# C probabilities turned by VectorE and a DRAM scratch array in all four halves, rows centred a pair ahead, rotations reordered

## What is computed

```python
h = x @ w_in                                  # split in ten column groups
a_out = pool_mixer(a_v, a_group_w, a_scale) * silu(a_gate)
b_out = sliding_window_attention(rope(b_q), rope(b_k), b_v, sinks) * silu(b_gate)
# C: 8 heads of 64; a chunk of 64 rows sees itself and the 8 chunks before it
s = (c_q @ c_k.T) * 64 ** -0.5 + rel_bias[h, clip(t - s, -128, 128)]
c_out = softmax(s) @ c_v * silu(c_gate)
y = concat(a_out, b_out, c_out) @ w_out
x = layer_norm(2 ** 0.5 * x + y) * ln_gain + ln_bias   # mean and deviation over the row
```

## Time and profile before

| | |
|---|---|
| median of three runs | 2816.25 us |
| the profiled execution | 2820.24 us, its span 2818.4 us |
| TensorE matmuls busy | 2783.0 us, 99% of the span |
| VectorE, ScalarE, GpSimd busy | 1827.0, 1271.7, 1278.3 us |
| granted clock of TensorE, mean | 0.997 |
| DMA moved | 427.09 MB, 152 GB/s over the span |
| chain that ended last | PE 88%, DVE 6%, DMA 3%, issue 1%, SPq 1%, ACT 1% |

### The profile page before, as it was taken

The page is one execution under the profiler, slowest core; times in us unless marked ns, Lnnn a source line. Parts: engine busy times, 40 slices in busy tenths (PEclk is TensorE's granted clock), DMA queues, the critical chain, the costliest instruction groups (busy, mean ns, idle before and its releaser), DMA issues.

```text
span 2818.4 us, 41183 instructions
## 1 busy us (share of the span) xinstructions
PE 2783.0 (99%) x12996; PEld 2322.1 (82%) x12996; DVE 1827.0 (65%) x2950; ACT 1271.7 (45%) x2628; POOL 1278.3 (45%) x927
## 2 busy tenths in 40 slices
PE   9999999999999999999999999999999999999998
PEld 7888888888888888888887878888888788788886
DVE  5666679623777777862267777896146778778625
ACT  4444466523444445652244445654234444456521
POOL 4444444444344434444444444444444444344441
PEclk9999999999999999999999999999999999999999
DMA  6555432355566533235577775334466777532442
GB/s 213 166 166 160 133 89 82 113 174 182 170 175 174 167 92 101 86 94 178 172 208 200 206 204 148 87 86 124 161 213 198 202 206 215 143 97 83 137 157 102
DMA packets 418502, 427.09 MB, mean 152 GB/s; under 512 B 215424, under 2 KB 256416, under 8 KB 414624
## 3 DMA queue, kind: packets, MB, share of 16 engines
q1 hardware_dynamic: 414544, 409.22, 49.4%
q10 hardware_dynamic: 3792, 15.73, 1.4%
HBM read 348.21 MB, written 79.78 MB: 152 GB/s over the span
## 4 chain that ended last, share of the span: by engine, by line
PE 88%; DVE 6%; DMA 3%; issue 1%; SPq 1%; ACT 1%; POOL 0%; DVEq 0%; ACTq 0%; POOLq 0%
PE acc L725 60%; PE sc L725 18%; PE pv L725 9%; DMA pt_raw<-c_prob_scratch 2%; PE sc L813 1%; DMA raw<-in_wall 1%; DVE mixl L1715 1%; DMA c_prob_scratch<-prob 1%; PE sc L769 1%; DVE res L1882 1%; DVE res L1891 1%; DVE mixh L1715 1%; DVE res L1894 1%; DVE pt L1715 0%; SPq L503 0%
## 5 line engine op out<-in xcount | busy, mean ns | idle before, releaser
L1682 POOL TENSOR_TENSOR wl<-raw,wh 128x512 fp32r<-128x512 f32 x920 | 1277.5, 1392 | 1496.8 <-ACT wh L1151 1486.7
L1151 ACT ACTIVATE wh<-raw 128x512 fp32r<-128x512 f32 x920 | 574.8, 630 | 1089.4 <-PE acc L725 747.5
L725 PE MATMUL acc<-xh,wh 128*128 128x512 f32 x2560 | 1007.7, 394 | 6.8 <-DVE mixl L1715 3.1
L725 PE MATMUL acc<-xh,wl 128*128 128x512 f32 x2560 | 998.3, 390 | 0.0
L725 PE MATMUL acc<-xl,wh 128*128 128x512 f32 x2560 | 998.2, 390 | 0.0
L725 PEld LDWEIGHTS acc<-xh,wh 128*128 128x128 f32 x2560 | 481.7, 188 | 103.7 <-DVE mixl L1715 4.4
L725 PEld LDWEIGHTS acc<-xh,wl 128*128 128x128 f32 x2560 | 480.9, 188 | 103.3
L725 PEld LDWEIGHTS acc<-xl,wh 128*128 128x128 f32 x2560 | 482.0, 188 | 92.3
L1715 DVE TENSOR_TENSOR xl<-prob,xh 128x512 f32 x48 | 55.9, 1165 | 237.3 <-ACT xh L1151 237.3
L725 PE MATMUL sc<-wh,mixh 128*128 128x512 f32 x496 | 193.5, 390 | 0.1
L725 PE MATMUL sc<-wl,mixh 128*128 128x512 f32 x496 | 193.0, 389 | 0.0
(11 more groups left out here) (233 smaller groups left out, 3724.4 us busy)
## 6 DMA issues: line engine op xcount, KB each, us to landing
raw<-in_wall SPq DMA_DIRECT2D x920, 256.0 KB, 2.7
res_scratch<-res ACTq DMA_DIRECT2D x12, 1024.0 KB, 4.2
res<-res_scratch SPq DMA_DIRECT2D x12, 1024.0 KB, 5.2
c_prob_scratch<-prob SPq DMA_DIRECT2D x64, 160.0 KB, 3.0
pt_raw<-c_prob_scratch SPq DMA_DIRECT2D x16, 640.0 KB, 5.0
res<-in_x SPq DMA_DIRECT2D x8, 1024.0 KB, 6.6
x_scratch<-res SPq DMA_DIRECT2D x8, 1024.0 KB, 5.2
x_t_scratch<-turned SPq DMA_DIRECT2D x128, 64.0 KB, 2.6
```

Of the source, the lines that this page charges most:

```text
L725: return nc.tensor.matmul(o, lhsT, rhs, start=start, stop=stop)
L1151: return nc.scalar.activation(o, i, ACT.Copy, scale=scale)
L1682: nc.gpsimd.tensor_tensor(wl[:, s, :], raw[:, s, :], wh[:, s, :].bitcast(F32), ALU.subtract).then_inc(w_lo, 1)
```

## The change

`on_tensor` is false for every half, so that half 1 runs `pair` and `second_half` with the scratch array (there with `turn_rows`, and `bias_rows` in ScalarE's `pair`). From pair 1 on, `load_ln` is issued at unit 1 in place of 8, and `centre` of pair p + 1 stands at the end of pair p; it waits for the sums alone, and `gain` for gain and bias. In the tail the rotations, the parts and the sums are reordered: in a second half `c_lo(2)` and `c_add(1)` now come after the first rotation rather than ahead of it, and `c_lo(3)` after the keys; in a first half `c_lo(3)` comes ahead of the second rotation. `rotated_keys` is the wait and the `keys_lo` that stood there before; the product of the C tail, and the parts made of it, come after the transpose of the B values.

```diff
@@ def on_tensor(it)
-            return it == 1
+            return False
@@ SyncE, pair_events
-                    if s == 8 and it:
-                        sp.wait_ge(w_used, unit(it, p * U_C) + (1 + RING))
+                    if it and s == (1 if p and not on_tensor(it) else 8):
+                        if s == 8:
+                            sp.wait_ge(w_used, unit(it, p * U_C) + (1 + RING))
                         load_ln(it - 1, p)
@@ ScalarE, pair
                     slot(12)
+                    if it == 1:
+                        bias_rows(1, p, tz_second)
@@ ScalarE, tail of a second half
                     c_hi(it, last, 2)
+                    query_hi()
                     split(it, KV0 + 7, 3)
-                    query_hi()
...
                     split(it, KV0 + 9, 1)
+                    b_keys_hi()
                     split(it, KV0 + 10, 2)
                     c_hi(it, last, 3)
                     split(it, KV0 + 11, 3)
-                    b_keys_hi()
...
                     b_query(it, 1, 1)
-                    mix_hi(nb + 2 * C_PAIRS, last + MIX_C)
...
                 split(it, B0 + 7, 3)
+                if not on_tensor(it):
+                    mix_hi(nb + 2 * C_PAIRS, last + MIX_C)
@@ VectorE
             def centre(it, n):
-                dv.wait_ge(ln_in, n * 48 + (192 * it + 48))
+                dv.wait_ge(ln_in, n * 48 + (192 * it + (16 if n and not on_tensor(it + 1) else 48)))
...
-            def gain():
+            def gain(it, n):
+                dv.wait_ge(ln_in, n * 48 + (192 * it + 48))
@@ first_half(p)
-                    if it:
+                    if it and p == 0:
                         centre(it - 1, p)
...
                     gate_ready(p * 2 + ((2 * C_PAIRS + B_TILES) * it + 2), 1)
+                    if it and p + 1 < C_PAIRS:
+                        centre(it - 1, p + 1)
@@ second_half(p)
-                    centre(it - 1, p)
+                    if p == 0:
+                        centre(it - 1, p)
                     low_keys(p)
-                    gain()
+                    gain(it - 1, p)
                     bias()
+                    if turns(it):
+                        turn_rows(it - 1, p)
                     low_values(p)
...
                     c_normalise(it, p, 2)
+                    if p + 1 < C_PAIRS:
+                        centre(it - 1, p + 1)
@@ VectorE, tail
                 rotate(it, 0, KV0 + 3, 0)
-                if not on_tensor(it):
-                    c_add(it, p, 2)
-                rotated_query(ROTS * it + 1, 0)
-                if half(it) and not on_tensor(it):
-                    c_lo(it, p, 3)
-                rotate(it, 1, KV0 + 7, 1, 1.0)
-                if not half(it):
-                    c_lo(it, p, 3)
...
+                elif half(it):
+                    c_lo(it, p, 2)
+                    c_add(it, p, 1)
+                    rotated_query(ROTS * it + 1, 0)
+                    rotate(it, 1, KV0 + 7, 1, 1.0)
+                    c_add(it, p, 2)
+                    rotated_keys()
+                    c_lo(it, p, 3)
+                else:
+                    rotated_query(ROTS * it + 1, 0)
+                    c_add(it, p, 2)
+                    c_lo(it, p, 3)
+                    rotate(it, 1, KV0 + 7, 1, 1.0)
+                    rotated_keys()
+                rotate(it, 2, B0 + 3, 1, source=q_bank)
                 if not on_tensor(it):
-                    c_tail_product(p, C_PAIRS * (it + 1))
-                dv.wait_ge(prod_ok, MIXES * it + 2 * C_PAIRS + 2)
+                    c_add(it, p, 3)
                 rotated_query(ROTS * it + 3, 1)
                 dv.wait_ge(w_used, unit(it, B0 + 7) + (1 + RING))
                 V.transpose(vals, v_bank).then_inc(vt_ok, 1)
                 if not on_tensor(it):
+                    c_tail_product(p, C_PAIRS * (it + 1))
+                    dv.wait_ge(prod_ok, MIXES * it + 2 * C_PAIRS + 2)
                     mix_lo(nb + 2 * C_PAIRS, p + MIX_C)
```

More of the change, by code:

```diff
@@ L2155, in _ @@
                     c_normalise(it, p, 3)
-                    c_lo(it, p, 2)
-                    c_add(it, p, 1)
                 elif not half(it):
@@ L2163, in _, with rotated_keys @@
                     c_lo(it, p, 2)
+                def rotated_keys():
+                    if half(it):
+                        dv.wait_ge(hist_mv, layer(it) + 1)
+                    dv.wait_ge(qh_ok, ROTS * it + 2)
+                    keys_lo([k[:, HD:] for k in bkl], s0[:, 0:HALF], [k[:, HD:] for k in bk]).then_inc(bq_ok, 1)
                 dv.wait_ge(rope_in, 32 * (it + 1))
                 rotate(it, 0, KV0 + 3, 0)
-                if not on_tensor(it):
-                    c_add(it, p, 2)
@@ L2178, in _ @@
-                if half(it) and not on_tensor(it):
-                    rotate(it, 2, B0 + 3, 1, source=q_bank)
-                    c_add(it, p, 3)
[L2181 to L2185, removed]
-                if not on_tensor(it):
-                    c_tail_product(p, C_PAIRS * (it + 1))
-                dv.wait_ge(prod_ok, MIXES * it + 2 * C_PAIRS + 2)
+                if on_tensor(it):
+                    rotated_query(ROTS * it + 1, 0)
[10 more added lines that the diff above has]
+                else:
+                    rotated_query(ROTS * it + 1, 0)
+                    c_add(it, p, 2)
+                    c_lo(it, p, 3)
+                    rotate(it, 1, KV0 + 7, 1, 1.0)
+                    rotated_keys()
```

## The result

The changed kernel takes 2851.97 us (median of four runs, 2851.25 to 2855.66) against 2817.64 for the kernel before beside it: ratio 1.012, 95% interval 1.0107 to 1.0134. It is slower by 34 us, far outside the forecast range (2803 to 2827). The profiled execution has a span of 2849.5 us, 31.1 longer than before.

A forecast was written before the change was run, and what follows sets the result against it. TensorE was taken as the bound. Half 0 -2.9, half 1 +2.8, half 2 -1.7 and half 3 +1.1 summed to -0.7 us, giving a median of 2815.5 us, with an 8-in-10 range of 2803 to 2827.

The forecast's parts named there:

- The bound: Whole kernel: TensorE, busy 2783.0 of 2818.4 us, so only shortening its stream or its few waits gains.
- Transposes, -17.5: Half 1: ten transposes fewer on TensorE per step, 1.09 us each over 16 steps, 17.5 us saved.
- Centring at the pair's end, halves 1 and 3, +7.5 each: Centring delays the gate: 2.95 us less 0.4 slack, 2.5 per pair, three pairs, +7.5 us in each half.
- rival B: Faster: new waits merge or centring does not collide with GpSimd; 12.3 us below, 2803; chance 0.30.
- rival D: Slower: every centring takes 3.87 us by the skill's exclusion rule, +9 us over nine places, 2824.5; chance 0.08.
- Half 1's queries, +5.1 and +2.9: Half 1: `turn_rows` delays the queries, 1.7 us in each of three pairs (+5.1) and +2.9 in pair 0.
- Half 1's waits for parts, +3.3: Half 1: waits for the C parts `pt`, put down to DMA latency and priced by half 3's, +3.3 us.
- Half 2, -8.3 + 6.6: Half 2: waits for keys and queries go (-8.3 us); centring delays `c_attend(1)` by 2.2 in three pairs (+6.6).
- `load_ln` earlier, 0: The 1 MB load, issued seven units earlier ahead of a pair's first scratch store, costs nothing.
- Rival C: Slower: the early 1 MB load delays the first scratch store and gate at nine pair ends, +13 us, 2829; chance 0.14.
- Tails: Reordered tails remove half 3's 3.48 us wait (-3.6 us) and half 0's 2.70 us wait (-2.9 us).
- The clock: Whole kernel: each TensorE wait priced at its idle time plus some 0.16 us overlap, nothing for a lower clock.

The follow-up runs named there:

- e1: The kernel before with half 1 alone moved to the scratch array, in the old order (centring in the middle of the pair): 2830.19 us, ratio 1.0044.
- e10: e9 with half 1 on the scratch array as well, no early load, turned rows still ahead of the queries: 2811.58 us, ratio 0.9972 to the kernel before.
- e12: e10 with half 1's gain moved out of the chain to the queries, ahead of the pooled values' low part: 2811.01 us, ratio 0.997 to the kernel before.
- e4: The changed kernel with the load of the sums at unit 4 instead of 1, behind the first scratch store: 2855.9 us, ratio 1.0139 to the kernel before.
- e7: The changed kernel with half 1's turned-row stores, pairs 0 to 2, issued behind the next pair's second scratch store: 2847.1 us, ratio 1.0093 to the kernel before.
- e3: The kernel before with only the changed kernel's reordered tails in halves 0, 2 and 3: 2816.45 us, ratio 0.9988.
- e2: The changed kernel with half 1 back on TensorE's transposes, the new order kept in halves 0, 2 and 3: 2830.34 us, ratio 1.0035 to the kernel before.
- e5: The kernel before with idle VectorE work in half 1 ahead of the queries' low parts, three maxima in pairs 0 and 1, six in 2 and 3: ratio 1.0095.
- e9: The kernel before with half 0's reordered tail, half 3's centring in VectorE's idle time, and half 3's tail with last C part before rotated keys: 2808.89 us, ratio 0.9965.
- e8: e9's edits plus half 2 reordered, keys' low parts ahead of bias and queries ahead of turned rows, on the kernel before: 2827.14 us, ratio 1.0022.

## Why the prediction was wrong

**The bound** was read rightly: TensorE, and what it waits for. Two steps failed: the price of half 1's waits for parts, taken from half 3 (3.3 us, measured 15.1), and the clock behind the waits, taken at nothing (some 20 us over the whole kernel). The others are gone through in their order.

**Transposes, -17.5:** no run gives it apart from the rest, but it fits. With it, what waits leave of half 1 is within 2.5 us of what its stretches under 1.00 add up to, in all eight rows of the table.

**Centring at the pair's end, halves 1 and 3, +7.5 each:** right in half 3. VectorE's row and TensorE's behind it:

```profile
2202.14 2.79 DVE L1885 TENSOR_SCALAR res<-res,mv,rstd 128x512 f32<-128x512 f32 x4
...
2209.24 0.68 DVE L1737 SCALAR_TENSOR_TENSOR gate<-gate,acc 128x512 f32<-128x512 f32 x1
...
2209.98 0.50 PE L726 MATMUL acc<-xh,wh 128*128 128x512 f32 x1 [2.19 <-DVE gate L1737]
```

2.79 us was taken as 2.95, and the waits are 2.34 with their overlap, three times, taken as 2.5. The gapless chain told it; rival B is out. The nine centrings at pair ends took 2.59 to 2.93 us, not 3.87, which puts rival D out, and with it the rule of the Trainium skill, SBUF — State Buffer, section Who interferes with whom, as a price for every centring. The single instructions of a centring took from 0.50 to 1.62 us; that the slow ones are those that meet GpSimd was not tested. In half 1 the step was priced far too dear: two of the three gates between pairs wait, 1.54 us each, and the tail's, priced at 1.5, not at all, since the attention products wait first. So +9.0 was forecast there and 3.1 came.

**Half 1's queries, +5.1 and +2.9:** 8.7 us, near in size, but with luck. The 0.96 us taken off for moving the centring were not there: e1 has it still in the middle and waits the same 2.18 us, and e10 has it elsewhere again and waits 2.17. What sets the wait is the chain from ScalarE's keys on, with gain, bias and turned rows (e10 to e12).

**Half 1's waits for parts, +3.3:** the first step that failed. They are 15.1 us with the tail's. I took half 3's, because "half 1 now runs as half 3 does". It does not: half 1 also stores 16 turned pieces per pair on the same queue, just ahead of the scratch. I had counted them only in the DMA share ("short of full"); 0.78 on the mean is short of full and says nothing of the 5.54 us at one store. The runs tell some of it apart. With the old order the parts cost 6.1 us (e1). The load of the sums ahead of the store made that store slow (e4), but to put the load (e4) or the turned rows' stores (e7) behind it did not lower half 1's waits; which transfer would have to go stays open. The tail's 3.72 us wait is e3's, the last part behind the keys.

**Half 2, -8.3 + 6.6:** the first term was exact. The second was three times 3.1 us, not 2.2: centring took 2.88 us, and the slack was none in any pair. To it comes 2.75 us for ScalarE's `prob`, behind the load of the sums.

```profile
1583.61 2.88 DVE L1885 TENSOR_SCALAR res<-res,mv,rstd 128x512 f32<-128x512 f32 x4
...
1588.67 0.68 DVE L1718 TENSOR_TENSOR pt<-pt_raw,pt 128x512 fp32r<-128x512 f32 x1
...
1589.49 0.77 PE L726 MATMUL pv<-pt,mixh 128*128 128x256 f32 x2 [2.98 <-DVE pt L1718]
```

**`load_ln` earlier, 0:** wrong in half 2 (the 2.75 us that e4 takes away) and in half 1 (the store's 5.5 us for 2.7, and `c_exp(1)`'s wait of 7.7 to 7.9 us for the 4.8 to 5.0 of e4), right in half 3, where SyncE was idle. Rival C had this mechanism, and its 2829 came nearer than my 2815.5, but it left out the clock and the parts.

**Tails:** half 0 -4.3 for -2.9. Half 3's L2191 wait went as forecast in the changed kernel; "what is next late" was named as the third rotation and is `c_lo(3)` (e3, e2 and half 1's tail; the changed kernel's half 3 got by with 1.04 us).

**The clock, never priced:** the second step that failed, and as large as the first. Every wait was costed at "the idle time named plus some 0.16 us". The kernel before shows otherwise: its wait of 2.70 us lies in a stretch of granted clock 0.91. Its removal brought 4.3 us, not the 2.9 of the wait. Half 1 lost 13.7 us by the clock, half 2 some 6 (10.5 less 3.8 of waits is 6.7, its stretches add up to 5.4), half 3 some 2. With waits alone the change would have come out at +11.5 us (29.0 more waits, less 17.5), just outside the range; the clock made it 31.

So the forecast set waits against transposes at their bare length. In half 1 the 27.8 us of waits cost half as much again by the clock.

## What to carry to other kernels

Price a wait of TensorE of 2 us and more at its length and, in a stream as dense as this one, at 1.4 us of clock besides: the changed kernel has sixteen, and its stretches in halves 1 to 3 lose 23.0 us in all, nothing behind five of them and up to some 2.8 behind one. Work spread in small steps, like these transposes, can be cheaper than the waits that replace it. Before a stage is costed by its sister's rows, list what else is issued on the same queue in this one and not in the other, and look at the one transfer that ends the wait, not at the mean share. When a wait is removed, ask what it gave time to, and what stands next: in e12 and e3 the next one was as long.

## What the runs showed that was not expected

A wait's second price grows much less than the wait: 3.78 us leave 3.4 us at the lower level, 5.96 us 4.6 and 5.0, since the clock falls inside the longer one (e5). In e9 waits of up to 1.5 us idle leave the granted clock at 1.00; at 2.0 us idle (e10) one wait does so and three are followed by 3.4 us at 0.50. The length does not decide alone: e10's wait of 1.32 us at 1672.34, behind a shorter one, is followed by 3.4 us at 0.50 too, and e7's of 3.12 us at 809.07 by none. Sixteen stores of 64 KB hold weights behind them for long enough to make ScalarE late by 4.05 us, at a mean DMA share of 0.78 (e8, 1600 to 1624 us).
